# Building the diagonal weights of a 31-tap convolution on GpSimd instead of ScalarE, with 11 taps on TensorE instead of 13, and splitting attention-stage weights in one piece

## What is computed

```python
h = x @ pw1_w + pw1_b
a, g = jnp.split(h, 2, axis=-1)
h = a * jax.nn.sigmoid(g)
h = causal_dwconv(h, dw_w, dw_b)      # 31 taps, per channel
h = silu(layer_norm(h, ln_g, ln_b))
return h @ pw2_w + pw2_b
```

## Time and profile before

| | |
|---|---|
| Time, median of 3 runs | 2185.11 us (2184.44 to 2187.16) |
| Profiled execution: its time | 2187.16 us |
| Profiled execution: its span | 2185.4 us |
| Mean granted TensorE clock, as a share of 2.4 GHz | 0.966 |
| PE busy | 2052.0 us (94%) |
| DVE busy | 1117.0 us (51%) |
| ACT busy | 776.8 us (36%) |
| POOL busy | 3.4 us |

### The profile page before, as it was taken

The page is one execution under the profiler, slowest core; times in us unless marked ns, Lnnn a source line. Parts: engine busy times, 40 slices in busy tenths (PEclk is TensorE's granted clock), DMA queues, the critical chain, the costliest instruction groups (busy, mean ns, idle before and its releaser), DMA issues.

```text
span 2185.4 us, 23202 instructions
## 1 busy us (share of the span) xinstructions
PE 2052.0 (94%) x8926; PEld 1610.8 (74%) x8926; DVE 1117.0 (51%) x1295; ACT 776.8 (36%) x1005; POOL 3.4 (0%) x24
## 2 busy tenths in 40 slices
PE   1999999999999899889999999989999999999996
PEld 0774678887788578566888888668777778888884
DVE  6674334225544498755555543354365555555433
ACT  2423233235522555425222221253365342222222
POOL 0000000000000000000000000000000000000000
PEclk8897999999999899999999999999999999999998
DMA  7211122221122111121222223212201222222321
GB/s 316 78 58 39 39 77 99 98 93 41 57 96 97 39 58 58 48 77 58 92 98 98 97 96 115 77 58 96 78 1 34 73 77 96 96 96 96 114 98 38
DMA packets 24830, 177.55 MB, mean 81 GB/s; under 512 B 2752, under 2 KB 2880, under 8 KB 4288
## 3 DMA queue, kind: packets, MB, share of 16 engines
q1 hardware_dynamic: 23040, 160.95, 20.7%
q10 hardware_dynamic: 1728, 15.73, 1.8%
HBM read 174.57 MB, written 2.10 MB: 81 GB/s over the span
## 4 chain that ended last, share of the span: by engine, by line
PE 87%; DVE 7%; ACT 4%; issue 1%; DMA 1%; DVEq 0%; ACTq 0%; SPq 0%
PE PS L407 23%; PE PS L408 23%; PE PS L409 23%; PE PS L482 3%; PE PS L762 2%; PE PS L772 2%; PE PS L471 1%; PE PS L473 1%; PE PS L472 1%; PE PS L590 1%; DVE ADAS L1232 1%; DVE TT L1187 1%; DMA SWR<-w_small 1%; PE PS L593 1%; PE PS L643 1%
## 5 line engine op out<-in xcount | busy, mean ns | idle before, releaser
L407 PE MATMUL PS<-H,WH 128*128 128x512 f32 x1552 | 614.1, 396 | 27.5 <-DVE L L1192 14.0
L408 PE MATMUL PS<-L,WH 128*128 128x512 f32 x1552 | 608.3, 392 | 0.0
L409 PE MATMUL PS<-H,WL 128*128 128x512 f32 x1552 | 607.9, 392 | 0.0
L1164 DVE TENSOR_TENSOR WL<-RAW,WH 128x2048 fp32r<-128x2048 f32 x145 | 332.1, 2291 | 312.2 <-ACT WH L801 311.7
L801 ACT ACTIVATE WH<-RAW 128x2048 fp32r<-128x2048 f32 x145 | 276.6, 1908 | 282.7 <-PE PS L409 237.6
L407 PEld LDWEIGHTS PS<-H,WH 128*128 128x128 f32 x1552 | 294.2, 190 | 96.7 <-issue 28.0
L409 PEld LDWEIGHTS PS<-H,WL 128*128 128x128 f32 x1552 | 293.8, 189 | 61.8
L408 PEld LDWEIGHTS PS<-L,WH 128*128 128x128 f32 x1552 | 294.1, 190 | 60.5 <-issue 0.2
L1080 ACT ACTIVATE TT<-TT 128x512 f32<-128x512 f32 x44 | 27.8, 632 | 310.2 <-DVE TT L1633 310.2
L407 PE MATMUL PS<-FH,WH 128*128 128x512 f32 x352 | 136.9, 389 | 0.0
L408 PE MATMUL PS<-FL,WH 128*128 128x512 f32 x352 | 136.9, 389 | 0.0
(11 more groups left out here) (285 smaller groups left out, 2616.1 us busy)
## 6 DMA issues: line engine op xcount, KB each, us to landing
RAW<-w SPq DMA_DIRECT2D x149, 1024.0 KB, 4.7
ADA<-w_ada ACTq DMA_DIRECT2D x8, 1536.0 KB, 23.8
X<-x_t SPq DMA_DIRECT2D x1, 2048.0 KB, 15.2
PWR<-w_ple ACTq DMA_DIRECT2D x2, 1024.0 KB, 4.8
out<-X SPq DMA_DIRECT2D x8, 256.0 KB, 2.2
PR<-p_t ACTq DMA_DIRECT2D x2, 512.0 KB, 5.7
PAR<-par SPq DMA_DIRECT2D x1, 334.0 KB, 7.1
SWR<-w_small SPq DMA_DIRECT2D x1, 160.0 KB, 18.9
```

The lines of the kernel that those rows point to most:

```text
L407: nc.tensor.matmul(ps, wh, xh, start=start, stop=False)
L408: nc.tensor.matmul(ps, wh, xl, start=False, stop=False)
L409: return nc.tensor.matmul(ps, wl, xh, start=False, stop=stop)
L1164: v.tensor_tensor(WL[:, p], RAW[:, p], WH[:, p].bitcast(F32), ALU.subtract).then_inc(w_lo, 1)
```

## The change

Two edits that are independent of each other.

In the convolution stage `PE_TAPS` goes from 13 to 11, so two more taps a chunk run on DVE. The diagonals are built by POOL with `tensor_scalar` (22 a chunk, all 8 chunks written out) from `DWC`, a small compact copy of the chunk's weights that DVE makes in each step just after `HC`. POOL waits for `dwc_ready`; ACT's `diagonals` goes, as do the waits on `cp_ps` and `dw_lo`.

In the attention stage each slot is split in one piece of 128x2048: ACT in step 2 of every 8 (before: halves in steps 1 and 2), DVE in step 2 too, ahead of the row maximum of that step (before: halves in steps 3 and 4).

```diff
-PE_TAPS = 13
+PE_TAPS = 11
...
-        CVB = at("CVB", A + 62, [P, 1, T])
-        DW = at("DW", A + 64, [P, 2, PE_TAPS * KC], F32R)
+        CVB = at("CVB", A + 60, [P, 1, T])
+        DW = at("DW", A + 62, [P, 2, PE_TAPS * KC], F32R)
+        DWC = at("DWC", A + 66, [P, 2, 2, PE_TAPS])
...
+            pool.wait_ge(const_ready, 6)
+
+            def diagonals(s):
+                p = s.odd()
+
+                pool.wait_ge(dwc_ready, s.val(1, 1))
+                for part in range(2):
+                    for k in range(PE_TAPS):
+                        ins = nc.gpsimd.tensor_scalar(DG[:, p, part, k, :], IDENT[:], DWC[:, p, part, k:k + 1], None,
+                                                      ALU.mult)
+                ins.then_inc(dg_ready, 1)
+            for m in range(KC):
+                diagonals(Step(m))
...
             for i in range(n + 2):
                 j = i // KC
-                if i % KC in (1, 2) and i < n:
-                    half_hi(SLOT0["za"] + j + 1, i % KC - 1)
+                if i % KC == 2 and i < n:
+                    split_hi(Step(j), 1, SLOT0["za"] + 1)
...
-            def diagonals(s):
-                p = s.odd()
-                if not (isinstance(s.val(), int) and s.val() < 2):
-                    act.wait_ge(cp_ps, s.val(1, -1))
-                for part in range(2):
-                    for k in range(PE_TAPS):
-                        m = s.val(1, k * KC)
-                        w_ = DW[:, part, m:m + 1] if isinstance(m, int) else DW[:, part, bass.ds(m, 1)]
-                        ins = a(DG[:, p, part, k, :], IDENT[:], ACT.Identity, scale=w_.bitcast(F32))
-                ins.then_inc(dg_ready, 1)
-
             def pw1(s, p):
-                if isinstance(s.val(), int) and s.val() == 0:
-                    act.wait_ge(dw_lo, 1)
-                diagonals(s)
                 gates("pw1", KC, "pw1_b")(s, p)
...
             for i in range(n + 1):
-                if i % KC in (3, 4) and i < n:
-                    half_lo(SLOT0["za"] + i // KC + 1, i % KC - 3)
+                if i % KC == 2:
+                    split_lo(Step(i // KC), 1, SLOT0["za"] + 1)
...
                 dve.wait_ge(bank_free, s.val(1, GROUP0["pw1"] + 1))
                 cv, hc = rows(CV, s.val(), 1), rows(HC, s.val(), 1)
-                q = s.odd()
+                q, m = s.odd(), s.val()
+                dw = DW[:].bitcast(F32).rearrange("p a (k m) -> p a k m", m=KC)
+
+                v.tensor_copy(DWC[:, q].unsqueeze(3), dw[:, :, :, m:m + 1] if isinstance(m, int) else
+                              dw[:, :, :, bass.ds(m, 1)]).then_inc(dwc_ready, 1)
+
```

More of the change, by code:

```diff
@@ L313, in build @@
         mg_ready, mg_hi, mg_lo = sem("mg_ready"), sem("mg_hi"), sem("mg_lo")
-        hc_hi, hc_lo, dw_hi, dw_lo, dg_ready, cp_ps = (sem(s) for s in (
-            "hc_hi", "hc_lo", "dw_hi", "dw_lo", "dg_ready", "cp_ps"))
+        hc_hi, hc_lo, dw_hi, dwc_ready, dg_ready, cp_ps = (sem(s) for s in (
+            "hc_hi", "hc_lo", "dw_hi", "dwc_ready", "dg_ready", "cp_ps"))
         sele_ready = sem("sele_ready")
@@ L1045, in pw1 @@
                 a(HCH[:, q:q + 1, :], rows(HC, s.val(), 1), ACT.Copy).then_inc(hc_hi, 1)
-            slots("pw1", pw1, head=2)
+            slots("pw1", pw1)
             act.wait_ge(sum_ready, LN_OF[N_CONV] + 1)
@@ L1506, in _ @@
             dve.wait_ge(dw_hi, 1)
-            v.tensor_tensor(DW[:, 1, :], col("dw_w", 0, PE_TAPS * KC), DW[:, 0, :].bitcast(F32),
-                            ALU.subtract).then_inc(dw_lo, 1)
+            own.did(v.tensor_tensor(DW[:, 1, :], col("dw_w", 0, PE_TAPS * KC), DW[:, 0, :].bitcast(F32), ALU.subtract))
+            own.settle()
             own.did(v.memset(acc, 0.0))
```

## The result

| | before | after |
|---|---|---|
| median of the runs | 2184.95 us (4 runs, 2184.44 to 2187.16) | 2218.68 us (4 runs, 2213.73 to 2220.39) |
| the profiled execution, its span | 2187.16, 2185.4 | 2214.47, 2212.7 |

The ratio is 1.0149, with a 95% interval from 1.0131 to 1.0167. The profiled execution is 27.3 us longer than that of before; the prediction's sum was 28.2.

A forecast was written before the change was run, and what follows sets the result against it. TensorE was busy 94% overall, but nearly tied with VectorE in the convolution stage. Terms -4.3 + 21 + 8.5 + 3.0 = +28.2 us on 2187.16 gave 2215.4, or 2213 us on the median; range 2200 to 2225.

The forecast's parts named there:

- Parts 1 to 3: Convolution stage: fewer TensorE taps, more VectorE work, no ScalarE diagonals ahead of the sigmoid; 4.3 us gained without GpSimd interference.
- Part 4, the company: Convolution steps: each of 176 GpSimd instructions delays a VectorE tap by 0.12 us, costing 21 us.
- Part 4, the tail: Convolution's end: chunk 7's diagonals come late with nothing covering them, and TensorE's clock is low; costs 8.5 us.
- Part 5, attention: Attention stage: row maxima come late behind ScalarE's whole-slot copy and VectorE's split; costs 3.0 us, bounds 0 and 5.
- Nobody disturbed: Rival, convolution stage: GpSimd does not disturb VectorE; 2184 us, no change; chance 0.17.
- Full block: Rival, convolution taps: each GpSimd instruction holds VectorE for all its 0.245 us; 2235 us; chance 0.22, shared with starved GpSimd.
- POOL is slowed, DVE is not: Rival, convolution: only the end pays, 8.5 us; 2192 us; chance 0.13, shared with GpSimd instructions long enough to set the pace.
- Faster: Rival: convolution start-up gain kept in full, GpSimd leaves VectorE alone, late attention maxima absorbed; 2179 to 2181 us; chance 0.10.

The follow-up runs named there:

- e3: Kernel before with 11 taps on TensorE instead of 13; diagonals stay on ScalarE, GpSimd does nothing, attention halves stay; 2186.06 us, ratio 1.0019.
- e8: Kernel before with ScalarE building each chunk's diagonals behind its sigmoid and HCH copy instead of ahead of the sigmoid, 13 taps; 2183.91 us, ratio 0.9998.
- e4: e3 plus 22 GpSimd products of 128x128 a chunk into scratch that nothing reads; 2203.66 us, ratio 1.0100.
- e7: Kernel after, but GpSimd reads DW itself, without VectorE's copies, and waits only until TensorE is done with the buffer; 2208.86 us, ratio 1.0116.
- e6: e3 plus 11 GpSimd products of 128x256 a chunk into scratch that nothing reads; 2209.66 us, ratio 1.0131.
- e11: e3 plus 22 GpSimd products of 128x64 a chunk into scratch that nothing reads; 2203.89 us, ratio 1.0087.
- e1: Kernel before with only the attention edit, each slot split in one piece by ScalarE and VectorE; 2190.77 us, ratio 1.0031.
- e12: Kernel before with only VectorE's low half of the slot split made whole, ScalarE's two halves kept; 2185.58 us, ratio 1.0011.
- e9: Kernel before with ScalarE's diagonals behind its sigmoid and HCH copy, and 12 taps on TensorE instead of 13; 2179.79 us, ratio 0.9987.

## Why the prediction was right, point by point

The parts stand against the profiled execution. The prediction's stage terms sum to 25.2 us; 24.8 were measured.

- **Parts 1 to 3**, -4.3 us with POOL disturbing nobody. ScalarE's block gone, chunk 0's `HC` comes 6.6 us after the `MEMSET`, not 10.9: 4.3 sooner, where 4.5 was said. VectorE becomes the bound: 18.7 to 18.9 in e3, 18.94 said. The copy of 22 values took 0.18, estimated at 0.15. Not foreseen: e3 and e8 show each gain of a few us hardly reaching the time.
- **Part 4, the company.** Taps 0.78 apart, as the sum had it, and the distance of `HC`s 21.1, said 21.6. The price per product is right at 0.12; 22 a step was too many, since the delay falls on the 18 two-input taps of a step. From chunk 0's `HC` to chunk 7's it is 148.3 us where the prediction's numbers give 150.6, 2.3 less, although the late diagonals of chunk 0 add 1.4 that it did not have. e4 shows the mechanism with no diagonal in it. But the size of 0.12 was luck. It was got as 0.245, the spacing of another instruction, less a gap of 0.12. The product itself takes 0.60 us with VectorE idle (e7), and the same reasoning with 0.60 would have made 0.48 a product and 84 us. Nor does it hold as a rule over the widths: it gives 0.37 for one of twice the length, and e6 has 0.24; it gives nothing below 128 columns, which is roughly what e11 shows. What is right is that the two engines take turns between instructions; that 0.12 us is the price was not known from any row of before.
- **Part 4, the tail.** Diagonals ready 18.9 us after `HC` (18.1 said), taps 10.1 (9.4 said, with 1.7 for the lower clock; it was 2.4). The wait of VectorE is 10.76. The last addition is 11.7 us later after the last `HC` than before, where the prediction's numbers give 10.0 (27.5 against 17.5). The 1.7 too little here and the 2.3 too much in the steps nearly cancel in the total, which is luck too. e7 took the tail away by timing alone.
- **Part 5, attention.** +3.0 said, +3.1 in e1's attention, +3.9 in the kernel after's, each known to 1 or 2 us. The row maximum is 4.2 us late (4.3 said), the next 1.1 (1.2 said), and TensorE's wait at the end of the chain 1.93 instead of 0.85. e12 shows that VectorE's whole half alone does not cost it: it takes the wait for ScalarE's whole copy.
- **The rivals.** "Nobody disturbed" falls by 0.78 against 0.66. "Full block", 0.91 apart, falls too, and more clearly than the prediction could see: with products of 0.60 us it would have set the taps 1.26 apart. The lock that the Trainium skill describes (page "SBUF — State Buffer", section "Who interferes with whom") is seen where a product meets a split (2.40 us for 0.60, e7); beside the taps VectorE pays only 0.12 a product, and GpSimd 0.20 on top of its 0.60. "POOL is slowed, DVE is not" is what e11 shows at 64 columns. "Faster" falls with both.

Open: why GpSimd is let in once per tap at 128 and 256 columns and every second time at 64; which part of a product's 0.60 us holds VectorE; and the cause of the lower clock behind the stage.

## What to carry to other kernels

An idle engine is not free room: ask what its instructions read and write beside the engine that sets the pace, and price that per instruction. Price it with a row of the same instruction, or say that there is none. Where work moves to a slower engine, look at the last chunk, in which nothing covers it, and at the first; starting it earlier mends that, and nothing else. And before moving work off an engine, try moving it down its queue: e9 got the whole start-up gain by placing ScalarE's diagonals behind the sigmoid, with one tap moved to even out the two engines.

## What the runs showed of the hardware

- VectorE's two-input taps and GpSimd's products take turns: 0.66 us apart alone, 0.78 with products of 128 columns, 0.90 with 256. With 64 columns VectorE is hardly delayed and GpSimd takes 1088 ns for what takes 442 alone.
- VectorE's split of 128x2048, with two SBUF inputs, held a GpSimd product until it was over: 2.40 us instead of 0.60 (e7).
- A GpSimd burst that only writes leaves two-input taps alone (0.66) but can hold a one-input `TENSOR_SCALAR` for the whole burst: 3.48 us instead of 0.56, in 3 of 8 steps of one profile.
- A product of 128x128 on GpSimd took 0.60 us with VectorE idle and 0.80 to 0.84 beside its taps, where its selects of the same size start 0.245 us apart.
- The same code behind the changed stage differed by 1.5 to 5 us over 1280, where gaps of TensorE let the clock fall to 1.2 GHz in one kernel and not in the other. On a kernel of this length a gain of 2 to 4 us in one stage can disappear there, so a stage is judged by its own length and the kernel by its ratio.
